# Feed-forward's first blocks: operand sums in the low parts' place, half by GpSimd, other banks, the spill in four pieces

## The reference, cut to what matters

```python
x = layer_norm(ALPHA * x + h @ w_out, ln1_g, ln1_b)     # (544, 2048)
u = jax.nn.relu(x @ w_up)                               # (544, 8192)
return layer_norm(ALPHA * x + (u * u) @ w_down, ln2_g, ln2_b)
```

## Time and profile before

| | us |
|---|---|
| median of the timed runs | 2782.72 |
| profiled execution, its own time | 2774.81 |
| profiled execution, its span (first to last instruction) | 2773.1 |
| TensorE busy in the span | 2686.1 |
| VectorE busy in the span | 1931.1 |
| ScalarE busy in the span | 1094.9 |
| GpSimd busy in the span | 339.3 |

### The profile page before, as it was taken

How to read it: one execution, slowest core, us unless ns; L and a number is a source line. 1 busy time by engine, 2 the same in 40 slices (tenths; PEclk the granted TensorE clock), 3 DMA queues, 4 the chain that set the end, 5 groups by cost and what they waited for, 6 DMA issues and landing times.

```text
span 2773.1 us, 58914 instructions
## 1 busy us (share of the span) xinstructions
PE 2686.1 (97%) x25059; PEld 2546.8 (92%) x25059; DVE 1931.1 (70%) x2366; ACT 1094.9 (39%) x1615; POOL 339.3 (12%) x357
## 2 busy tenths in 40 slices
PE   8999999999999898899999999999998999999998
PEld 8998988888899667799989999999998999999997
DVE  3374554554554386787987787788777888888887
ACT  3221221222221375445535555555553333333331
POOL 3011101111010131111102222222220000000000
PEclk9999999999999999999999999999999999999999
DMA  7889999999999862377536666666678757565732
GB/s 241 295 315 403 413 407 412 405 409 406 411 405 373 301 201 98 104 211 203 149 118 204 189 202 180 199 192 193 188 235 278 242 180 239 161 218 173 235 98 95
DMA packets 542216, 691.84 MB, mean 249 GB/s; under 512 B 25723, under 2 KB 467164, under 8 KB 531538
## 3 DMA queue, kind: packets, MB, share of 16 engines
q1 hardware_dynamic: 465042, 477.59, 52.2%
q0 software_dynamic: 13872, 141.28, 12.5%
q10 hardware_dynamic: 63040, 69.21, 7.3%
HBM read 589.21 MB, written 98.79 MB: 248 GB/s over the span
## 4 chain that ended last, share of the span: by engine, by line
PE 47%; DVE 1%; DMA 1%; SPq 1%; issue 0%; ACT 0%; DVEq 0%; ACTq 0%
PE big_G L2390 15%; PE big_G L2392 15%; PE big_G L2391 15%; DMA raw<-in_w_down 1%; PE big_G L2499 1%; SPq L2245 0%; DMA raw<-in_w_up 0%; PE big_G L2495 0%; PE big_G L2497 0%; PE big_G L2496 0%; DVE raw L2679 0%; DVE wl L2667 0%; DVE base L2679 0%; SPq L2261 0%; DVE big_xl L2687 0%
## 5 line engine op out<-in xcount | busy, mean ns | idle before, releaser
L472 PE MATMUL prj_G<-prj_xh,prj_wh 128*128 128x280 f32 (+1 forms) x1696 | 500.5, 295 | 1.7 <-issue 1.7
L474 PE MATMUL prj_G<-prj_xh,prj_wl 128*128 128x280 f32 (+1 forms) x1696 | 495.2, 292 | 0.0
L473 PE MATMUL prj_G<-prj_xl,prj_wh 128*128 128x280 f32 (+1 forms) x1696 | 494.2, 291 | 0.0
L727 DVE STREAM_TRANSPOSE prj_kT<-base 128x4096 f32<-128x4096 f32 x64 | 284.4, 4444 | 259.3 <-PE prj_S L505 259.3
L2528 ACT ACTIVATE wh<-raw 128x768 fp32r<-128x768 f32 (+1 forms) x294 | 279.6, 951 | 373.0 <-PE big_G L2392 199.4
L2667 DVE TENSOR_TENSOR wl<-raw,wh 128x768 fp32r<-128x768 f32 (+1 forms) x294 | 329.6, 1124 | 119.8 <-ACT wh L2528 119.6
L472 PEld LDWEIGHTS prj_G<-prj_xh,prj_wh 128*128 128x128 f32 x1696 | 321.3, 189 | 25.9 <-issue 24.4
L2390 PE MATMUL big_G<-big_xh,wh 128*128 128x272 f32 x1168 | 338.7, 290 | 3.4 <-ACT base L2531 1.7
L2392 PE MATMUL big_G<-big_xh,wl 128*128 128x272 f32 x1168 | 338.2, 290 | 0.0
L2391 PE MATMUL big_G<-big_xl,wh 128*128 128x272 f32 x1168 | 336.5, 288 | 0.0
L2390 PE MATMUL big_G<-ff_window,wh 128*128 128x272 f32 x1116 | 322.6, 289 | 7.1 <-DVE wl L2667 7.1
(11 more groups left out here) (484 smaller groups left out, 6035.2 us busy)
## 6 DMA issues: line engine op xcount, KB each, us to landing
prj_v_nat<-in_cache_v SPq DMA_DIRECT2D x242, 512.0 KB, 8.1
raw<-in_w_up SPq DMA_DIRECT2D x128, 512.0 KB, 4.4
u_scratch<-base SPq DMA_DIRECT2D x60, 952.0 KB, 6.6
ff_window<-u_scratch SPq DMA_DIRECT2D x70, 816.0 KB, 7.3
prj_raw<-in_w_in ACTq DMA_DIRECT2D x103, 512.0 KB, 17.8
raw<-in_w_down SPq DMA_DIRECT2D x120, 384.0 KB, 4.7
raw<-in_w_out SPq DMA_DIRECT2D x60, 512.0 KB, 4.9
ff_left_over<-in_w_down SPq DMA_DIRECT2D x80, 192.0 KB, 6.4
```

The source lines that it names most:

```text
L472: mm(out, w_hi[:, k, m], xh[:, k0 + k, cols], start=(first and k == 0), stop=False)
L473: mm(out, w_hi[:, k, m], xl[:, k0 + k, cols], start=False, stop=False)
L474: last = mm(out, w_lo[:, k, m], xh[:, k0 + k, cols], start=False, stop=(end and k == nk - 1))
L727: V.transpose(flat(kT[:, :, :, :, :].rearrange("p r h b i -> p r (h b i)")), flat(k_nat[k % 2][:, :, :]))\
```

## The change: what it does

1. T2, T3 and T4 are no longer made in `u2` but in the place where their low parts go afterwards (`WHOLE`), so no sum has to wait until the one before it has been used. VectorE makes T2 and T4; GpSimd makes all four column pairs of T3, at the stage's start and without a wait, and all four of T1, once `up_plain` is done.
2. `up_plain` writes `G[2]` and `G[3]`, and no longer waits for ScalarE's copies; `down_first` writes `G[0]` and `G[1]`; every `seven(g)` uses the other pair of banks than before.
3. The spill of `y` goes in four DMAs of four tiles each. The last four tiles go first, when the adds are done; the other three go behind loads of the next block's weights on SP's queue. Whoever waited for the spill waits for all four.

```diff
-                    if h == 0:
-                        pe.wait_ge(copied, m + 1)
...
+            def spill_y(i):
+                rows = slice(KT // NSPILL * i, KT // NSPILL * (i + 1))
+                sp.dma_start(dram["y_scratch"][:, rows, :], y[:, rows, :]).then_inc(y_out, 16)
+
             sp.wait_ge(y_done, FIRST_ADDS)
-            sp.dma_start(dram["y_scratch"], y).then_inc(y_out, 16)
+            spill_y(3)
             for g in range(NUP - 1):
                 sp.wait_ge(lo_done, base_of(g) + 5)
                 load_role(g + 1, 0)
+                if g == 0:
+                    spill_y(0)
                 sp.wait_ge(sum_done, sums_of(g) + 4)
                 load_role(g + 1, 3)
+                if g == 0:
+                    spill_y(1)
                 sp.wait_ge(lo_done, base_of(g) + 6)
                 load_role(g + 1, 2)
+                if g == 0:
+                    spill_y(2)
...
                 if b <= 2:
-                    ac.wait_ge(y_out, 16)
+                    ac.wait_ge(y_out, 16 * NSPILL)
...
             for kp in range(4):
-                a, b = (two(u2[:, (kp + i) % 2, :]) for i in range(2))
...
+                third, second = (pair(WHOLE, x, kp) for x in (T3, T2))
+                dv.wait_ge(third_made, kp + 1)
+                make(T2, third, part(0, kp), ALU.add, kp)
+                dv.wait_ge(made_here, 2 * kp + 1)
+                make(T4, part(2, kp), second, ALU.subtract, kp)
+                turn_low(T3, kp, 3 * kp + 1)
+                dv.wait_ge(made_here, 2 * kp + 2)
+                turn_low(T2, kp, 3 * kp + 2)
+                turn_low(T4, kp, 3 * kp + 3)
+                low(3 + kp, Q[BY_FREE[(3 + kp) % 4]])
+            for t in range(3):
+                add_first(t)
+            for kp in range(4):
+                first_low(kp)
+                add_first(3 + kp)
...
+            for kp in range(4):
+                G_.tensor_tensor(pair(WHOLE, T3, kp), part(3, kp), part(1, kp), ALU.subtract).then_inc(third_made, 1)
+            po.wait_ge(up_done, DOWN)
+            for kp in range(4):
+                G_.tensor_tensor(pair(WHOLE, T1, kp), part(1, kp), part(0, kp), ALU.subtract).then_inc(first_made, 1)
             for b in range(1, NUP + 1):
                 po.wait_ge(relu_done, b + 1)
                 if b == 1:
-                    po.wait_ge(y_out, 16)
+                    po.wait_ge(y_out, 16 * NSPILL)
```

More of the change, by code:

```diff
@@ L2068, in over @@
             return nc.alloc_sbuf_tensor_at("ff_" + name, shape, dt, offset=at)
+        for x in (T1, T2, T3, T4):
+            WHOLE[x] = over(f"whole{x}", [P, KH, W], region + (COMBO_AT[x] + 1) * COMBO)[:, :, :]
         NARROW, GAP = CH * P, (KH - CH) * P
@@ L2154, in sums_of @@
         def sums_of(g):
-            return NSUM + 4 * g
+            return 4 * g
         def five_at(g, role):
@@ L2212, in banks_of @@
         def banks_of(g):
-            return [G[2 * (g % 2) + i // 2][:, i % 2, 0:W] for i in range(4)]
+            return [G[2 * ((g + 1) % 2) + i // 2][:, i % 2, 0:W] for i in range(4)]
         def y_adds(v):
@@ L2398, in up_plain @@
                     m, h = q // 2, q % 2
-                    if h == 0:
-                        pe.wait_ge(copied, m + 1)
                     for c in range(2):
                         for k in range(KH):
-                            last = third(G[m][:, c, 0:HALF_M], ring_h[n % RING][:, k, :], ring_l[n % RING][:, k, :], HI[2 * h + c][:, k, :],
+                            last = third(G[2 + m][:, c, 0:HALF_M], ring_h[n % RING][:, k, :], ring_l[n % RING][:, k, :], HI[2 * h + c][:, k, :],
                                          LO[2 * h + c][:, k, :], h == 0 and k == 0, h == 1 and k == KH - 1)
@@ L2418, in down_first @@
                             pe.wait_ge(y_done, t - 1)
+                        else:
+                            pe.wait_ge(copied, t + 1)
                         for c, cols in enumerate(HALVES):
                             for k in range(FB):
-                                last = third(G[2 + t % 2][:, c, 0:HALF_M], w_hi[:, k, i * P:(i + 1) * P], w_lo[:, k, i * P:(i + 1) * P],
+                                last = third(G[t % 2][:, c, 0:HALF_M], w_hi[:, k, i * P:(i + 1) * P], w_lo[:, k, i * P:(i + 1) * P],
                                              uh[:, k, cols], ul[:, k, cols], k == 0, k == FB - 1)
@@ L2531, in take, with turn_high @@
                 A(two(out), G[m][:, :, 0:HALF_M], ACT.Copy).then_inc(copied, 1)
-            def turn_high(x, temp, kp, sums):
-                ac.wait_ge(sum_done, sums)
-                A(pair(HI, x, kp), temp, ACT.Copy).then_inc(turned, 1)
+            def turn_high(x, kp, made, times):
+                ac.wait_ge(made, times)
+                A(pair(HI, x, kp), pair(WHOLE, x, kp), ACT.Copy).then_inc(turned, 1)
             for m in range(2):
@@ L2554, in _ @@
             ac.wait_ge(up_done, DOWN)
+            ac.wait_ge(low_done, 1)
+            for m in range(2):
+                take(2 + m, u2[:, 1 - m, :])
             for kp in range(4):
-                turn_high(T1, two(u2[:, kp % 2, :]), kp, 13 + kp)
+                turn_high(T1, kp, first_made, kp + 1)
             ac.wait_ge(raw_full[BY_FREE[3]], 16)
             high(7, Q[BY_FREE[3]])
-            ac.wait_ge(low_done, NLOW)
-            for m in range(2):
-                take(m, u2[:, 1 - m, :])
             def high_of(g, n):
@@ L2675, in add_first @@
                 out = two(y[:, first_tile(t), :])
-                V.scalar_tensor_tensor(out, G[2 + t % 2][:, :, 0:HALF_M], 1.0 / ALPHA, out, ALU.mult, ALU.add).then_inc(y_done, 1)
+                V.scalar_tensor_tensor(out, G[t % 2][:, :, 0:HALF_M], 1.0 / ALPHA, out, ALU.mult, ALU.add).then_inc(y_done, 1)
             def combine(out, in0, in1, op):
@@ L2682, in accumulate, with make, turn_low @@
                 V.tensor_tensor(out, out, in1, ALU.add).then_inc(added, 1)
-            def turn_low(x, temp, kp, n):
+            def make(x, in0, in1, op, kp):
+                V.tensor_tensor(pair(WHOLE, x, kp), in0, in1, op).then_inc(made_here, 1)
+            def turn_low(x, kp, n):
                 dv.wait_ge(turned, n)
[L2687 to L2691, removed]
+                V.tensor_tensor(pair(LO, x, kp), pair(WHOLE, x, kp), pair(HI, x, kp).bitcast(F32), ALU.subtract).then_inc(low_done, 1)
             def first_low(kp):
-                turn_low(T1, two(u2[:, kp % 2, :]), kp, 13 + kp)
+                turn_low(T1, kp, 13 + kp)
             def low_of(g, n):
@@ L2733, in _ @@
             for kp in range(4):
[L2734 to L2764, removed]
+                third, second = (pair(WHOLE, x, kp) for x in (T3, T2))
[13 more added lines that the diff above has]
+                add_first(3 + kp)
             low(7, Q[BY_FREE[3]])
-            add_first(6)
+            add_first(7)
             dv.wait_ge(copied, 4)
             relu_square(u2)
-            for t in (7, 8):
-                add_first(t)
+            add_first(8)
             low_of(0, 0)
```

16 lines of the change are left out of this document (9 added, 7 removed).

## The result

The changed kernel takes 2800.21 us, the median of 15 runs (2785.93 to 2807.74), beside 2786.99 us for the kernel before on the same chip (15 runs, 2776.32 to 2795.9). The medians lie 13.2 us apart; the ratio of the two series is 1.0043 with an interval of 1.0029 to 1.0057, which on 2786.99 is slower by 12.0 us (8 to 16). The forecast was +13.2 us on 2782.7, that is 2796; the 15 runs of the kernel before have a median 4.3 us above that of the three runs it was reckoned from.

What follows compares the result with a forecast made beforehand. TensorE, busy 97% of the span, was taken as the bound. The terms 0.5 + 1.5 + 9.7 + 1.5 = +13.2 us on the timed median 2782.7 gave 2796 us, range 2786 to 2801.

Steps and rivals of the forecast that it cites:

- the two mechanisms: GpSimd's sums and VectorE's two-SBUF-input operations exclude each other; spill pieces behind weight loads land 10.5 us later.
- The start: `up_plain`, no longer waiting for ScalarE's copies, lets TensorE start at 1388.2, 0.6 us earlier (between 0 and 1.7).
- VectorE's hold-up: Before the first add, GpSimd's sums and VectorE's operations take turns; TensorE waits 7.9 us, spending the whole gain: +0.5 us.
- T0: Start of `seven(0)`, 1443.65 before; forecast 1444.1 (+0.5 us), plus 1.5 for the clock, near 1446.
- the clock: After TensorE's 7.9 us wait on the first add, the granted clock drops towards 1.2 GHz: +1.5 us (0 to 2).
- for the tightest steps: 1 us added to the 48.0 us of `up_plain` and `down_first` when taking VectorE's sums alone, giving 1437.2 for T0.
- The spill: Its last quarter, behind three weight loads, lands at T0 + 25.7; the second operand of `seven(1)` comes +9.7 us (8 to 11).
- The clock behind it: After TensorE's 11.7 us wait in `seven(1)`, the lower clock again costs +1.5 us.
- The signs it named: After-profile: stretched VectorE operations, one 6 to 8 us first-add wait, T0 near 1446, late spill, 11 to 12 us wait in `seven(1)`.
- the case without hold-up: Rival, chance 0.22: GpSimd and VectorE don't delay each other; T0 is 1437.2, total +4.8 us, 2787.5.
- the case in which the spill no longer decides: Rival, chance 0.04: all pieces land by T0 + 14, the `seven(1)` wait goes, full gain 8.4 us: 2774.

Runs made afterwards that it cites:

- e3: Changed kernel with the spill in one DMA and all sixteen operand sums on VectorE, none on GpSimd; ratio to the kernel before 0.9970.
- e7: Changed kernel with the spill in one DMA and each GpSimd sum replaced by three memsets; stage 125.44 us against 131.67 in the kernel before.
- e1: Changed kernel with the spill in one DMA again, issued after the 16 adds, ahead of the weight loads; ratio to the kernel before 0.9988.
- e2: Kernel before with only the spill cut into four pieces, in the change's places on SP's queue; ratio to the kernel before 1.0053.
- e8: Changed kernel where GpSimd and ScalarE each wait only for the spill pieces whose room they take; stage 137.59 us against 131.67 before.
- e6: Changed kernel with 88 throwaway matmuls on TensorE ahead of the second product of `seven(1)`; stage 141.77 us against 143.46 in the changed kernel.
- e4: Changed kernel with each of the four spill pieces issued as soon as its four tiles have their adds; ratio to the kernel before 0.9987.
- e5: Changed kernel with all operand sums on VectorE and the four spill pieces issued as soon as their adds are done; ratio to before 0.9975.

## Why the prediction was right, point by point

The direction and the two mechanisms held, and the size came out close: +13.2 us forecast, +12.0 timed, +11.79 in the stage. How close is in part luck: one term missed by -3.0 us and two others by +1.6 together. By its steps:

- **The start.** Forecast 1388.2. Measured 1403.20 - 15.03 = 1388.17.
- **VectorE's hold-up.** Right as a mechanism (e3, e7), but mis-sized. The prediction took 1.4 us for a GpSimd sum of 544 columns, as the price of one hold. A hold cost 2.39 - 1.22 = 1.17 us, and a GpSimd sum alone takes 1.37 us (the least of the four below), so part of it overlaps. And only three of the four T1 sums came ahead of the first add, not four: the last runs until 1427.75 + 7.31 = 1435.06, beside two adds that take 1.34 us together, no longer than two of 0.72 each. An add reads `G` in PSUM and only one operand in SBUF. So the first round began 0.85 us earlier than forecast (1397.55, not 1398.4), three rounds took 0.5 less (4.43 us each, not 4.6), the fourth, with three holds and not four, 2.3 less (1433.79 - 1425.88 = 7.9, not 10.2): the first add came at 1418.8, not 1422.4, and TensorE waited 3.86 us, not 7.9. GpSimd's four T3 sums, as a group by source line (ns: least, median, most):

```profile
L2942 POOL TENSOR_TENSOR ff_whole<-base x4: 1372/2382/2417, 1403.1 to 1409.2; 128x544 f32<-128x544 f32 x4
```

- **T0** was therefore 1.04 us earlier than before, where the prediction had 0.5 + 1.5 = 2.0 later. This is the one term with the wrong sign: 3.0 us off, 3.6 by the first add, less 0.6 behind it: the 14 tiles took 1457.64 - 1434.56 = 23.1 us, where 21.0 + 1.5 for the clock was forecast. The clock was forecast rightly: the first 14 matmuls of the restart took 1437.86 - 1434.56 = 3.30 us, and 14 matmuls behind the second wait before, at clock 1.00, 1471.53 - 1469.66 = 1.87; that is 1.4 us. The other 0.6 us was lost in the tiles behind, at a clock of 1.00: the prediction counts 1 us "for the tightest steps" where it takes VectorE's sums alone, and leaves it out here. In e3, where the clock stayed at 1.00, the 14 tiles took 22.0 us. TensorE's timeline before, 14 matmuls behind that wait:

```profile
1471.53 0.29 PE L2392 MATMUL big_G<-big_xh,wl 128*128 128x272 f32 x1
```

- **The spill.** Forecast to land at T0 + 25.7; GpSimd was let go at T0 + 26.7 (before 15.2 and 15.3). The operand came 36.66 us after T0 instead of 26.01, +10.65 where +9.7 was forecast. The wait was 12.28 us (11.7). e1, e2 and e8 show that this term comes from the pieces' places alone.
- **The clock behind it.** Forecast +1.5; measured 2.2 in this trace (e6), 1.5 and 1.4 in e2 and e8.
- **The signs it named.** The spill's landing, the wait in `seven(1)` and the clock behind it (0.50) came as named, and the start. Three did not: VectorE's relu-square wasn't stretched beside GpSimd (1.35 us, before 1.29), the wait on the first add was 3.86 us and not 6 to 8, and T0 was 1457.64 - 15.03 = 1442.6 and not near 1446.

In sum -1.04 + 10.65 + 2.18 = +11.79: the T0 term missed by -3.0, the other two by +0.95 and +0.7. Against the rivals: e3 is the case without hold-up, and its stage (-5.65 with one spill) lies near the -6.4 us that the prediction gave T0 there (T0 itself came 5.60 earlier); e4 and e5 are the case in which the spill no longer decides, and land on the side of faster, as the prediction had it for that case: 8.4 us worked out with all waits gone, 7.01 measured in e5.

By parts, from e1 and e3: sums in their own place and other banks -5.65 us; GpSimd's share of them +4.56; the pieces' places +12.88; together +11.79. The sums' place, the banks and the order of the adds that came with them were not taken apart; the earlier start is 0.7 us of the -5.65.

## What to carry to other kernels

When a transfer that somebody waits for is cut into pieces on an ordered queue, its end is that of the last piece with everything queued ahead of it: start the pieces earlier, don't put them behind loads that wait for buffers. Work moved from VectorE to GpSimd is not off VectorE when GpSimd reads SBUF beside VectorE's operations with two SBUF inputs: eight sums of 0.72 us were taken away, and six holds of 1.17 us came back. A wait of TensorE is to be counted with the slow restart behind it, here 1.4 us for a wait of 3.9 us and 2.2 for one of 12.3.

## What the runs showed of the hardware that was not expected

- VectorE and GpSimd took turns while both read two SBUF operands, at 1.17 us for each GpSimd sum of 128 x 544; beside GpSimd's fills (1.16 us for two) and for VectorE's adds with a PSUM operand nothing was lost.
- What the lower clock cost did not follow the length of the wait: 1.4 us behind 3.86 and 7.20 us of waiting, 1.5 behind 12.70, 2.2 behind 12.28. After waits of up to 2.0 us it had stayed at 1.00.
- An issue on SP's queue took 3.4 us instead of 0.4 where several transfers were already in flight. (So it did before, up to 3.43 us for the weight loads behind the spill.) In e4, whose last three pieces leave 6 us apart, each took 0.37 us.
